# Convolution taps that add up in the PSUM bank, and another order of steps in the first input product

## The reference

```python
# first block
z = rms_norm(x, norm_mix) @ w_in          # 22 column tiles of 128
y_a = lru mixer:  xc = causal_dwconv(xr, conv_w[4]) + conv_b; gates r, i = sigmoid(xb @ w + b)
                  h = scan(a * h + b);  y = h * gelu(gate)
y_b = bg * causal_dwconv(cg * xs, sc_conv_w[3])       # short convolution
y_c = attention with forget gates (4 heads of 64)
y_d = attention over compressed, selected and windowed keys (31 compressed keys: a product over
      32 x 64 inputs, gelu, a second product, softmax)
x = x + concat(rms_norm(y_*)) @ w_out
gu = rms_norm(x) @ w_gate_up;  x = x + (silu(gu[:F]) * gu[F:]) @ w_down        # F = 2816
# second model, 4 layers: mixer (convolution, neighbourhood attention, retention, convolution), then
def conv_ffn(h, w_up, dw_w, dw_b, w_down):
    u = dwconv(h @ w_up, dw_w, dw_b)          # 3 taps over time, each of 5632 channels by itself
    val, gate = split(u)
    return (gelu(gate) * val) @ w_down
```

## Time and profile before

| | us |
|---|---|
| median of 3 runs | 3274.71 |
| the profiled execution | 3271.2 |
| its span, first to last instruction | 3269.4 |
| PE busy | 3180.6 |
| DVE busy | 1914.0 |
| POOL busy | 1563.7 |
| ACT busy | 1118.1 |

### The profile page before, as it was taken

One profiled execution on the slowest core, in us unless ns is written; L12 is line 12 of the kernel. 1 busy time (PEld: TensorE's weight loads), 2 busy tenths in 40 slices (PEclk: granted clock), 3 DMA queues, 4 the chain that ended last, 5 costly groups with the idle time before them and its releaser, 6 DMA issues. The chain is left out here.

```text
span 3269.4 us, 34977 instructions
## 1 busy us (share of the span) xinstructions
PE 3180.6 (97%) x13869; PEld 2454.7 (75%) x13869; DVE 1914.0 (59%) x2862; ACT 1118.1 (34%) x1674; POOL 1563.7 (48%) x764
## 2 busy tenths in 40 slices
PE   8889999999999999999999999999999999899999
PEld 5657888875778877778788777777878876587887
DVE  5465111289685585447675833322767588876756
ACT  5453222255422224553222322222322235532222
POOL 3224555567354553334545534443454557545454
PEclk9999999999999999999999999999999999999999
DMA  4212333321233333222323322222232332123232
GB/s 179 70 44 78 99 95 97 101 67 58 68 95 96 97 97 106 88 78 78 103 88 94 104 81 71 78 78 71 86 101 90 97 97 65 39 90 103 85 96 91
DMA packets 80675, 286.03 MB, mean 87 GB/s; under 512 B 9088, under 2 KB 9344, under 8 KB 80384
## 3 DMA queue, kind: packets, MB, share of 16 engines
q1 hardware_dynamic: 80512, 283.80, 27.3%
HBM read 281.40 MB, written 2.10 MB: 87 GB/s over the span
## 5 line engine op out<-in xcount | busy, mean ns | idle before, releaser
L2205 POOL TENSOR_TENSOR WL<-RAW,WH 128x1024 fp32r<-128x1024 f32 x504 | 1238.4, 2460 | 1321.3 <-ACT WH L1533 1320.8
L1301 PE MATMUL PS<-XH,WH 128*128 128x512 f32 x2640 | 1081.3, 410 | 29.2 <-POOL WL L2205 23.2
L1303 PE MATMUL PS<-XH,WL 128*128 128x512 f32 x2640 | 1032.5, 391 | 0.0
L1302 PE MATMUL PS<-XL,WH 128*128 128x512 f32 x2640 | 1031.5, 391 | 0.0
L1533 ACT ACTIVATE WH<-RAW 128x1024 fp32r<-128x1024 f32 x504 | 527.4, 1049 | 520.5 <-PE PS L1303 432.2
L1301 PEld LDWEIGHTS PS<-XH,WH 128*128 128x128 f32 x2640 | 497.2, 188 | 200.0 <-issue 74.5
L1302 PEld LDWEIGHTS PS<-XL,WH 128*128 128x128 f32 x2640 | 497.9, 189 | 110.5 <-issue 16.3
L1303 PEld LDWEIGHTS PS<-XH,WL 128*128 128x128 f32 x2640 | 497.0, 188 | 107.0
L1301 PE MATMUL PS<-HH,WH 128*128 128x512 f32 x1264 | 498.9, 395 | 11.2 <-DVE HL L2103 9.6
L1303 PE MATMUL PS<-HH,WL 128*128 128x512 f32 x1264 | 493.6, 390 | 0.0
L1302 PE MATMUL PS<-HL,WH 128*128 128x512 f32 x1264 | 493.4, 390 | 0.0
(11 more groups left out here) (226 smaller groups left out, 2511.7 us busy)
## 6 DMA issues: line engine op xcount, KB each, us to landing
RAW<-wst SPq DMA_DIRECT2D x504, 512.0 KB, 3.5
BI<-natb SPq DMA_DIRECT2D x16, 384.0 KB, 4.6
X<-xin SPq DMA_DIRECT2D x16, 256.0 KB, 4.7
X<-cmpw SPq DMA_DIRECT2D x1, 2048.0 KB, 9.5
out<-X SPq DMA_DIRECT2D x8, 256.0 KB, 2.0
BI<-relm SPq DMA_DIRECT2D x4, 448.0 KB, 9.8
PRM<-prm SPq DMA_DIRECT2D x1, 685.0 KB, 12.2
BI<-rope SPq DMA_DIRECT2D x2, 256.0 KB, 4.0
```

What stands on the lines that cost most here:

```text
L1301: e.matmul(o, wh, h, start=first, stop=False)
L1302: e.matmul(o, wh, l, start=False, stop=False)
L1303: t = e.matmul(o, wl, h, start=False, stop=last)
L2205: e.tensor_tensor(WL[:, b % NSPLIT, :], RAW[:, b % NRAW, :], WH[:, b % NSPLIT, :].bitcast(f32), SUB).then_inc(*did(lo_made, ("lo", b)))
```

## The change

The taps. `scaled_in` is `scaled` without freeing the bank. In the convolved feed-forward the bank is scaled into the padded tile as before; then ACT writes the centre tap with its bias from the padded tile into the bank the tile came from, and DVE adds the two neighbours there, with the bank as input and output. GELU reads the bank and writes a tile (`gelu_from`), and a value tile is multiplied out of the bank into the tile of its gate (`times_bank`). The bank is freed after that. LRU and short convolution do the same; their last DVE tap of the LRU writes the tile `xc`, and the short convolution's three products with b, c and x read the bank.

The order. `soon` is now sorted by due time. `head_norm` is due 5 weight tiles after its tile (3 before), the LRU step 8 (3 before), the swap 7 (4 before). In a beat values, turn and normalisation come ahead of the scores. `cmp_blocks` is four steps `cmp_block`, 2, 6, 10 and 14 weight tiles after their tile, the four products are due at 22 to 25 (12 before) and the next step at 28. The softmax of the compressed scores is a step of its own, `cmp_soft`, in beat 4; `cmp_turn` stays in beat 6.

```diff
@@ -292,7 +292,14 @@
             def later(fn, delay=3, first=False):
-                (soon if first else bg).append((state["tile"] + delay, fn))
+                due = state["tile"] + delay
+                if not first:
+                    bg.append((due, fn))
+                    return
+                n = len(soon)
+                while n and soon[n - 1][0] > due:
+                    n -= 1
+                soon.insert(n, (due, fn))
 
...
@@ -425,7 +437,7 @@
                     bank.done((j, "hn"))
-                later(go, first=True)
+                later(go, 5, first=True)
                 return got
...
@@ -497,14 +509,14 @@
                     def f():
-                        if n < len(units):
-                            scores(n)
                         if 0 <= n - 3 < len(units):
...
                             normalise(n - 1)
+                        if n < len(units):
+                            scores(n)
                         if n in beside:
...
@@ -543,12 +555,13 @@
                 step("clear", pad.ap[:, 0:3], pad.free)
-                z = scaled(pad.ap[:, 3:515], bank, n_mix, made)
-                i = step("taps", xc.ap, xc.free, pad.ap, z, "lru_conv_w", c, 2, 4, pcol("lru_conv_b", c))
+                z = scaled_in(pad.ap[:, 3:515], bank, n_mix, made)
+                i = step("taps", xc.ap, xc.free, bank.ap, pad.ap, z, "lru_conv_w", c, 2, 4, pcol("lru_conv_b", c))
                 pad.done((i, "taps"))
+                bank.done((i, "taps"))
                 st["lru", c] = (xc, tiles.get(), tiles.get(), (i, "taps"))
                 if c == 1:
-                    later(lru_gates, first=True)
+                    later(lru_gates, 8, first=True)
 
...
@@ -606,13 +619,14 @@
                 step("clear", pad.ap[:, 0:2], pad.free)
-                z = scaled(pad.ap[:, 2:514], bank, n_mix, made)
+                z = scaled_in(bank.ap, bank, n_mix, made)
                 cb = st["c", c][0]
-                i = step("times", pad.ap[:, 2:514], cb.ap, z, st["c", c][1])
-                i = step("taps", cb.ap, (), pad.ap, (i, "m"), "sc_conv_w", c, 2, 3, None)
+                i = step("times_bank", pad.ap[:, 2:514], bank.ap, cb.ap, (z, st["c", c][1]))
+                i = step("taps", bank.ap, (), bank.ap, pad.ap, (i, "m"), "sc_conv_w", c, 2, 3, 0.0)
                 pad.done((i, "taps"))
                 bb, b_made = st["b", c]
-                i = step("times", cb.ap, bb.ap, (i, "taps"), b_made)
+                i = step("times_bank", cb.ap, bank.ap, bb.ap, ((i, "taps"), b_made))
+                bank.done((i, "m"))
                 bb.done((i, "m"))
...
@@ -699,15 +713,23 @@
                     blk = [tiles.get() for _ in range(4)]
-                    i0 = step("cmp_blocks", b.ap, z, [s.ap for s in blk], [x for s in blk for x in s.free])
-                    b.done((i0, "blk"))
+                    laid = {}
+
+                    def block(l0):
+                        def f():
+                            s = blk[l0 // 8]
+                            i = step("cmp_block", l0, b.ap, z, s.ap, s.free)
+                            laid[l0] = (i, "blk")
+                            if l0 == 24:
+                                b.done((i, "blk"))
+                        return f
 
...
                             bk = st["cb"]
-                            i = step("cmp_product", l0, bk.ap, bk.free, blk[l0 // 8].ap, (i0, "blk"))
+                            i = step("cmp_product", l0, bk.ap, bk.free, blk[l0 // 8].ap, laid[l0])
                             if l0 < 24:
...
@@ -742,8 +764,10 @@
                     for l0 in range(0, 32, 8):
-                        later(product(l0), 12)
-                    later(go)
+                        later(block(l0), 2 + l0 // 2, first=True)
+                    for l0 in range(0, 32, 8):
+                        later(product(l0), 22 + l0 // 8)
+                    later(go, 28)
                 elif j == 1:
...
@@ -775,14 +799,18 @@
 
+                def cmp_soft():
+                    sc, sm, rc, made = cmp["a"]
+                    i = step("cmp_soft", c, sc.ap, sm, rc, made, st["gt"])
+                    cmp["a"] = (sc, (i, "p"))
+
                 def cmp_turn():
-                    sc, sm, rc, made = cmp["a"]
+                    sc, made = cmp["a"]
                     bks, pcs = [], []
...
                         pcs.append(pads.get())
-                    i = step("cmp_turn", c, sc.ap, sm, rc, made, st["gt"], [(bk.ap, bk.free) for bk in bks],
-                             [(pc.ap, pc.free) for pc in pcs])
+                    i = step("cmp_turn", sc.ap, made, [(bk.ap, bk.free) for bk in bks], [(pc.ap, pc.free) for pc in pcs])
                     for p in range(2):
...
@@ -819,7 +847,7 @@
                             ob=out, start=(u, br) == (3, 0), stop=False, after=after if (u, br) == (0, 1) else None))
-                attend(units, (4, 3)[c], {1: cmp_scores, 6: cmp_turn, 10: cmp_values})
+                attend(units, (4, 3)[c], {1: cmp_scores, 4: cmp_soft, 6: cmp_turn, 10: cmp_values})
 
...
@@ -857,18 +885,26 @@
                     b = tiles.get()
-                    pair(m, b, scaled(b.ap, bank, norm, made, b.free), "silu")
+                    pair(m, b, scaled(b.ap, bank, norm, made, b.free))
 
...
                     step("clear", pad.ap[:, 513:514], ())
-                    z = scaled(pad.ap[:, 1:513], bank, norm, made)
-                    b = tiles.get()
-                    i = step("ffn_taps", b.ap, b.free, pad.ap, z, layer, ch)
+                    z = scaled_in(pad.ap[:, 1:513], bank, norm, made)
+                    i = step("ffn_taps", bank.ap, pad.ap, z, layer, ch)
                     pad.done((i, "taps"))
-                    pair(m, b, (i, "taps"), "gelu")
+                    if m % 2 == 0:
+                        b = tiles.get()
+                        j = step("gelu_from", b.ap, b.free, bank.ap, (i, "taps"))
+                        bank.done((j, "f"))
+                        cur["g"] = (b, (j, "f"))
+                    else:
+                        b, g_made = cur["g"]
+                        j = step("times_bank", b.ap, bank.ap, b.ap, (g_made, (i, "taps")))
+                        bank.done((j, "m"))
+                        hid[m // 2] = split_to(m // 2, b.ap, (j, "m"), b)
 
...
@@ -1616,6 +1652,23 @@
 
+            def gelu_from(i, b, b_free, bank, made):
+                table[0] = ACT.Gelu_apprx_tanh
+                for event in b_free:
+                    w.wait_ge(*at(event))
+                w.wait_ge(*at(made))
+                e.activation(b, bank, ACT.Gelu_apprx_tanh).then_inc(*did(act_made, (i, "f")))
+
+            def taps(i, o, free, bank, src, made, name, c, nch, n, bias):
+                w.wait_ge(*at(made))
+                e.activation(bank, src[:, n - 1:n - 1 + T], ACT.Identity, scale=pcol(name, (n - 1) * nch + c),
+                             bias=bias).then_inc(*did(act_made, (i, n - 1)))
+
+            def ffn_taps(i, bank, pad, made, layer, ch):
+                w.wait_ge(*at(made))
+                e.activation(bank, pad[:, 1:513], ACT.Identity, scale=pcol("ffn_dw_w", 132 * layer + 44 + ch),
+                             bias=pcol("ffn_dw_b", 44 * layer + ch)).then_inc(*did(act_made, (i, "c")))
+
             def silu(i, b, made):
...
@@ -1859,20 +1912,18 @@
 
-            def taps(i, o, free, src, made, name, c, nch, n, bias):
+            def taps(i, o, free, bank, src, made, name, c, nch, n, bias):
                 for event in free:
                     w.wait_ge(*at(event))
-                w.wait_ge(*at(made))
-                if bias is None:
-                    e.tensor_scalar(o, src[:, n - 1:n - 1 + T], pcol(name, (n - 1) * nch + c), None, MUL).then_inc(
-                        *did(dve_made, (i, n - 1)))
-                else:
-                    e.tensor_scalar(o, src[:, n - 1:n - 1 + T], pcol(name, (n - 1) * nch + c), bias, MUL,
-                                    ADD).then_inc(*did(dve_made, (i, n - 1)))
                 for j in range(n - 2, -1, -1):
                     w.wait_ge(*at((i, j + 1)))
-                    e.scalar_tensor_tensor(o, src[:, j:j + T], pcol(name, j * nch + c), o, MUL, ADD).then_inc(
-                        *did(dve_made, (i, j), *(() if j else ((i, "taps"),))))
+                    e.scalar_tensor_tensor(bank if j else o, src[:, j:j + T], pcol(name, j * nch + c), bank, MUL,
+                                           ADD).then_inc(*did(dve_made, (i, j), *(() if j else ((i, "taps"),))))
+
+            def times_bank(i, o, bank, b, after):
+                for event in after:
+                    w.wait_ge(*at(event))
+                e.tensor_tensor(o, bank, b, MUL).then_inc(*did(dve_made, (i, "m")))
 
...
@@ -1968,24 +2019,20 @@
 
-            def cmp_blocks(i, b, made, blk, free):
+            def cmp_block(i, l0, b, made, blk, free):
                 pos = PRM[:, POFF["cmp_pos"]:POFF["cmp_pos"] + 32]
...
```

(47 more changed lines are left out.)

10 lines of the change are left out of this document (5 added, 5 removed).

## The result

The changed kernel takes **3223.9 us** (median of 4 runs, 3222.0 to 3224.5) against 3274.6 for the kernel before on the same chip (4 runs): a ratio of 0.984 (0.983 to 0.986), 50.7 us less. The forecast was 3220, 54 us less. The profiled execution took 3222.0 us by its own time (span 3220.2), 49.2 less than the 3271.2 of the one before. The same kernel timed once more later gave 3220.6 (5 runs, ratio 0.984, 0.982 to 0.985).

The account below looks back on a forecast made before the run. PE was taken to bound the kernel, through waits, late matmul starts and halved clock. Gains of 32.8 + 20.3 + 1.2 = 54.3 us from 3271.2 gave 3216.9, plus 3.5 for the median 3220.4, or 3220 us; range 3203 to 3248.

Parts of the forecast that it names:

- What bounds: Whole kernel: PE, busy 97% of the span; edits off PE regain only waits, late matmuls inside busy, and halved clock.
- Feed-forward taps: Four convolved feed-forward stages: bank taps of 0.75 us let them run as the plain one, 32.8 us less.
- rival (b): Feed-forward: bank taps as long as SBUF taps, DVE still 11.4 us per pair, only 21.5 us come: 3253; chance 0.06.
- Rival (c): Feed-forward: DVE and ACT in lock-step through every tile, 12.1 us a pair, 3315 us in all; chance 0.04.
- Rival (d): Centre taps: function in another table than GELU, two loads of 1.28 us per pair, 3228 us; chance 0.05.
- First product: First product, 176 weight tiles: reordered steps remove PE waits and clock dips, 20.3 us less, bounds 5 and 32.
- waits of before gone: First product: PE waits of 6.1, 5.8, 1.2, 2.3 and 1.4 us go, 16.8 in all.
- new at tiles 96, 97: First product: compressed scores in the second beat need a norm issued at 95; new wait 0.8 us (0 to 3).
- LRU region, new: First product, tile 124: new PE wait of 4.4 us for the turned copy, then 1.2 and 1.3 for normalisations.
- clock: First product: two of three half-clock stretches go with their waits, 4.5 us less; the third stays.
- the forced scan: First product, tile 120: 4 buffers free where 7 are asked, so the first LRU scan follows at once, ahead of beat 121.
- Neighbourhood layer: Neighbourhood layer: head norms due later, so its one PE wait for them goes, 1.2 us less.

Follow-up runs that it names:

- the SBUF form: Changed kernel, but in the feed-forward ACT's centre tap and DVE's two neighbour taps add up in an SBUF tile: 3274.9 us, ratio 1.0006.
- without the force: Changed kernel, but nothing forced out from tile 104 on while 2 buffers are spare, gates with roots left as they are: 3222.5 us, ratio 0.984.

## Why the prediction was right, step by step

**What bounds.** PE, through waits, late starts inside "busy", and a halved clock. Right: removing off-PE work changed the time only where one of the three was, and the convolved stages stopped exactly at the plain one's 359.9.

**Feed-forward taps: 32.8 forecast, 32.7 measured.** The bank tap at 0.75, read from 268 rows of another layer, decided it; rival (b) is out. The case reads one thing better than the forecast did: there I argued mainly from the sum of DVE's work (4.9 us a pair). A fall in DVE's work alone does not do it; the SBUF form had less work than before and was slower. For the kernel before, the sum was right as far as it went: DVE had almost no gap. But much of that was blocked time, part of it in the centre tap, to which the forecast gave no price: 1.12 us on average, 0.55 when free. DVE's busy time of 148 against the "near 120" that I named: 22 pairs of 5.1 are 112, and the stage's DVE work outside its pairs, some 36 us (an estimate, from the plain stage's 80.4 less 22 pairs of two scalings and a product), I had left out.

**Rival (c), lock-step.** It did not come, because its condition, a bank tap of 1.45 us or more, is not met. But its mechanism is real, in the SBUF form: 11.87 us a pair (forecast for it: 12.1), enough to eat the whole gain of the new order (3274.9 against 3255.2).

**Rival (d), table loads.** None came: L1669, 176 times, is preceded by no load (35 loads in all, before and after), and the convolved stage has 165 ACT instructions against 121 in the plain one, exactly 44 centres more.

**First product: 20.3 forecast, 19.5 measured.** By the step's own terms:

| term | forecast | measured |
|---|---|---|
| waits of before gone | 16.8 | 16.8 |
| norm wait at tile 27, now 29 | 2.0 to 0.6 | 2.0 to 0.6 |
| new at tiles 96, 97 | 0.8 | 0 |
| new at tile 83 | not foreseen | 1.3 |
| LRU region, new | 4.4 + 1.2 + 1.3 = 6.9 | 5.5 + 1.9 = 7.4 |
| clock | 4.5 | 2 of 3 low stretches gone; PE's busy time 225.2 to 221.1, 4.1 less |

The waits give 16.8 + 1.4 - 1.3 - (7.4 - 5.3) = 14.8, and with one of 0.5 at tile 142 that went too, 15.3; by the windows PE is idle for 15.4 us less and busy for 4.1 less, together the 19.5. The wait for the copy was mis-sized by 1.1. From the first gate product at 164.25, PE came after 8.2 us (forecast 7.8) and the copy was ready after 13.6 (12.2). Two errors stand against one another in the 12.2. I let ACT start with PE, and it began 2.0 us later, at 166.24, behind a beat's exponentials and two copies (L1756). And its work was sized wrongly: the durations that I listed add up to 12.6 us before the copy and 13.1 with it, while ACT took 11.6 for all of it, because its instructions overlap (gate functions of 0.69 us start 0.57 to 0.61 apart). The blame on the forced scan was wrong in the main: without the force 1.2 us of the copy's wait goes and 0.6 comes back elsewhere. The wait at tile 83 was missed because I followed only the steps whose due times changed most. It is there in the run with the new order alone and not in the one with the new taps alone. Just ahead of it on DVE stand a head norm's scaling, now later, and one of the four compression pieces (104.23 to 106.73); which of them makes it, no run tells apart.

**Neighbourhood layer: 1.2 forecast, none measured.** The failed step is "its one wait goes", taken as the whole effect of the later place. The wait went and the first group is 1.4 us shorter, but the same later place costs 0.2 us in each of the seven groups after it, a term that the forecast put at nothing. Which instruction is late in them the table of waits doesn't show.

**Left out: 3.0 us given back elsewhere.** "Convolution and retention layers keep their order: nothing." By the profiled executions the convolution layers are 2.5 longer, with other stretches at low clock. For the second layer that cannot be laid to the change: it is 2.8 shorter in the second execution of the same kernel. The first layer is open: it took 205.3 us before and 206.7 in both executions of the changed kernel, and 206.2 to 208.0 in the nine other runs, those with only one of the two parts included; but the kernel before was profiled once. The medians were 50.7 below the kernel before in the first timing and 53.0 (3273.6 to 3220.6) in the second, so that the forecast's 54.3 is 1 to 4 us too high.

## What to carry to other kernels

Look at an element-wise chain's slow instances behind its engine's busy share: DVE's 98% in a stretch of the kernel before was in good part blocked time, and with the same taps still on DVE, but in the bank, 62% remained (40.8 of 65.3 us). If the same instruction takes 0.75 us in one place and 2.8 in another, find what runs beside it and move an operand out of SBUF before moving work to another engine. Work moved to another engine changes who is released together with whom, and can line the blocked instructions up. A wait that is taken away from a schedule that is 98% busy counts only when the stage's window has become shorter; several here moved on to a later tile, and one came back as 0.2 us in each of seven groups.

## What was not expected of the hardware

- Blocked taps end 0.55 us after GpSimd's instruction, whatever they had done before it ended: 2.29 and 2.58 us for taps that began 0.67 and 0.36 us into its 2.4 us. Free, the same form takes 0.752, and a tap that had begun before GpSimd's instruction did was not blocked: 68 such in the kernel before (L2048) have a mean of 0.752.
- A tap with its accumulator in PSUM takes 755 ns, one with it in SBUF that isn't blocked 752: the bank has no price of its own in this form. VectorE's centre tap, another form, takes 813 ns into a bank and 547 into SBUF when free, but 1121 on average there (L2045), since it was often blocked.
- The centre on ACT takes 783 ns and on DVE, the same write into a bank, 813.
- The granted clock fell to its lower level (0.50) in the convolution layers for 3.4 to 10.2 us at a time, at different points in executions of one program, without any different wait: 2.8 us in one stage.
